# Three output tiles on each normed k-tile, a final norm in token layout, an earlier first weight unit and one table set for log and exp, in a hybrid transformer trunk of depth 2

## The reference, cut to what matters

```python
def rms_norm(x, g):
    x32 = x.astype(F32)
    y = x32 * lax.rsqrt(jnp.mean(x32 * x32, axis=-1, keepdims=True) + NORM_EPS)
    return y.astype(x.dtype) * g

def adaln(cond, w, b):
    m = jax.nn.silu(cond) @ w + b
    return jnp.split(m, 6, axis=-1)

def swiglu(h, w1, w3, w2):
    return (jax.nn.silu(h @ w1) * (h @ w3)) @ w2

# per layer: sh, sc, g of the mixer and of the FFN come from adaln
#   x = x + g1 * (mixer(rms_norm(x, norm1_g) * (1 + sc1) + sh1) @ w_out)
#   x = x + g2 * swiglu(rms_norm(x, norm2_g) * (1 + sc2) + sh2)
# at the end: y = rms_norm(x, final_norm_g), for both token groups
```

## Time and profile before

| what | us |
|---|---|
| median of three runs | 1251.12 (1247.42 to 1253.12) |
| the profiled execution | 1250.76 |
| its span | 1248.9 |
| PE busy with matmuls | 1154.1 |
| POOL, DVE, ACT busy | 541.0, 444.4, 430.8 |

### The profile page before, as it was taken

How to read it: one execution, slowest core, us unless ns; L and a number is a source line. 1 busy time by engine, 2 the same in 40 slices (tenths; PEclk the granted TensorE clock), 3 DMA queues, 4 the chain that set the end, 5 groups by cost and what they waited for, 6 DMA issues and landing times.

```text
span 1248.9 us, 17436 instructions
## 1 busy us (share of the span) xinstructions
PE 1154.1 (92%) x7238; PEld 1047.4 (84%) x7238; DVE 444.4 (36%) x822; ACT 430.8 (34%) x658; POOL 541.0 (43%) x414
## 2 busy tenths in 40 slices
PE   5699998999988999999999989778998999999997
PEld 3399898977767999999999869565597999999996
DVE  4523899215766311111111230428655101111112
ACT  0442422452343423322222242447615333323222
POOL 0344588330015364554455524113043565565662
PEclk9599999989999999999999979889998999999998
DMA  9743323345234666655566642042025444434331
GB/s 311 252 127 104 101 68 102 118 136 189 82 85 138 180 188 185 187 169 170 164 202 184 173 158 68 17 119 68 1 68 135 111 125 135 121 105 117 116 117 51
DMA packets 242940, 163.84 MB, mean 131 GB/s; under 512 B 20214, under 2 KB 241453, under 8 KB 242862
## 3 DMA queue, kind: packets, MB, share of 16 engines
q1 hardware_dynamic: 214880, 135.74, 37.5%
q10 hardware_dynamic: 27982, 26.99, 6.9%
HBM read 159.81 MB, written 2.90 MB: 130 GB/s over the span
## 4 chain that ended last, share of the span: by engine, by line
PE 74%; DVE 12%; ACT 5%; DMA 3%; POOL 3%; issue 2%; ACTq 0%; SPq 0%; DVEq 0%
PE banks L410 19%; PE banks L412 18%; PE banks L411 18%; POOL w_lo L1014 3%; PE banks L484 3%; ACT w_hi L1038 2%; DVE ht L1467 1%; PE banks L450 1%; PE banks L452 1%; PE banks L451 1%; DMA raw<-in_ada_w 1%; DVE h_lo L1458 1%; DVE Qd L1635 1%; DMA raw<-in_w_in_even 1%; DVE Kd L1635 1%
## 5 line engine op out<-in xcount | busy, mean ns | idle before, releaser
L1014 POOL TENSOR_TENSOR w_lo<-raw,w_hi 128x512 fp32r<-128x512 f32 (+2 forms) x410 | 540.8, 1349 | 685.3 <-ACT w_hi L1038 685.3
L410 PE MATMUL banks<-h_hi,w_hi 128*128 128x384 f32 x1152 | 394.6, 343 | 24.4 <-DVE h_lo L1458 16.7
L411 PE MATMUL banks<-h_lo,w_hi 128*128 128x384 f32 x1152 | 388.8, 338 | 0.0
L412 PE MATMUL banks<-h_hi,w_lo 128*128 128x384 f32 x1152 | 388.7, 337 | 0.0
L1038 ACT ACTIVATE w_hi<-raw 128x2048 fp32r<-128x2048 f32 (+4 forms) x115 | 193.4, 1682 | 206.3 <-PE banks L412 157.8
L410 PEld LDWEIGHTS banks<-h_hi,w_hi 128*128 128x128 f32 x1152 | 218.5, 190 | 37.9 <-issue 30.7
L411 PEld LDWEIGHTS banks<-h_lo,w_hi 128*128 128x128 f32 x1152 | 218.7, 190 | 0.7
L412 PEld LDWEIGHTS banks<-h_hi,w_lo 128*128 128x128 f32 x1152 | 218.3, 190 | 0.6
L1510 DVE TENSOR_TENSOR uf<-sa,banks 128x384 f32<-128x384 f32 x44 | 24.4, 554 | 330.2 <-PE banks L412 324.2
L410 PE MATMUL banks<-u_hi,w_hi 128*128 128x384 f32 x352 | 118.8, 338 | 0.9 <-POOL w_lo L1014 0.9
L412 PE MATMUL banks<-u_hi,w_lo 128*128 128x384 f32 x352 | 117.7, 334 | 0.0
(11 more groups left out here) (348 smaller groups left out, 1288.2 us busy)
## 6 DMA issues: line engine op xcount, KB each, us to landing
raw<-in_ffn_w SPq DMA_DIRECT2D x88, 512.0 KB, 5.2
raw<-in_ada_w SPq DMA_DIRECT2D x28, 1024.0 KB, 5.9
raw<-in_ffn_w SPq DMA_DIRECT2D x32, 704.0 KB, 4.6
vada_raw<-in_ada_w ACTq DMA_DIRECT2D x20, 1024.0 KB, 6.7
raw<-in_w_in_even SPq DMA_DIRECT2D x18, 1024.0 KB, 5.2
raw<-in_w_out_even SPq DMA_DIRECT2D x4, 1024.0 KB, 5.7
raw<-in_w_in_odd SPq DMA_DIRECT2D x3, 1024.0 KB, 7.3
raw<-in_w_in_odd SPq DMA_DIRECT2D x8, 256.0 KB, 4.4
```

Source lines behind the costliest of these rows:

```text
L410: pe.matmul(out, s_hi, m_hi, start=first and j == 0, stop=False)
L411: pe.matmul(out, s_hi, m_lo, start=False, stop=False)
L412: mm = pe.matmul(out, s_lo, m_hi, start=False, stop=last and j == len(terms) - 1)
L1014: ins = pool.tensor_tensor(w_lo[s % SPLIT][:, at:to], raw[u % RAW][:, at:to], w_hi[s % SPLIT][:, at:to].bitcast(F32), ALU.subtract)
```

## The change

It has four parts.

1. `first_features` takes three tiles instead of two: in `out0` and `out1` output tiles 0 to 2, in the FFNs gate 0, up 0 and gate 1, in `in1` three `qc` tiles. In `in0` there are still two. The third tile comes from the next unit, `u + 1`. The line that releases unit `u` is unchanged: it names the second tile's completion.
2. The final norm: X's tile m-1 is transposed (`turn_y`, 3 transposes) right after down tile m of layer 1, and DVE multiplies it by the gain row (`take_y`) into `y_tok`, laid over `vada_raw`. `final_norm_g` is broadcast to all partitions by a DMA on ACT's queue. At the end the sum of squares is taken by 6 matmuls with one column each, so the mean stands with tokens on the partitions (128 x 3), and `rstd` scales three rows of 1024: one on ACT, two on DVE, each followed by a DMA.
3. The order at the start: the first `in0` unit ahead of the fourth modulation pair, the second `in0` unit ahead of "norm0"; PE makes modulation "norm0" ahead of the fifth tile of `in0`; DVE and ACT do the lower-bound chain after the norm; ACT splits the second unit after the norm.
4. `norm` loads one table set, `natural_log_exp_and_others`, in place of the dummy log. Over the program ACT has 20 table loads in place of 28.

```diff
-    ada("start")
+    ada("start", range(0, 3))
     add("in0", 1, DT, 256)
+    ada("start", range(3, 4))
+    add("in0", 1, DT, 256, 1)
     ada("norm0")
-    add("in0", 6, DT, 256, 1)
+    add("in0", 5, DT, 256, 2)
...
                 outs = [dense.fill(pe, key)[:, 0:T] for key in keys]
-                unit_ready(u)
                 for k in range(DT):
-                    pe.wait_ge(S["h_ready"], ready + k + 1)
                     for i, out in enumerate(outs):
-                        mm = three(out, [(*weight(u, DT, k, i * P), h_hi[:, k, :], h_lo[:, k, :])], k == 0, k == DT - 1)
+                        if k == 0 and i % 2 == 0:
+                            unit_ready(u + i // 2)
+                        if i == 0:
+                            pe.wait_ge(S["h_ready"], ready + k + 1)
+                        mm = three(out, [(*weight(u + i // 2, DT, k, i % 2 * P), h_hi[:, k, :], h_lo[:, k, :])],
+                                   k == 0, k == DT - 1)
                         if k == DT - 1:
                             mm.then_inc(dense.done, 1)
                 release[u] = (dense.done, dense.at[keys[1]] + 1)
...
+            def turn_y(m):
+
+                dense.was_read(pe, ("down", 1, m))
+                turn(misc, ("y", m), [(c * P, X[:, m, c * P:(c + 1) * P]) for c in range(NCH)])
+
...
-                first_features([("gate", l, 0), ("up", l, 0)], number[(f"up{l}", 0)], ready)
+                first_features([("gate", l, 0), ("up", l, 0), ("gate", l, 1)], number[(f"up{l}", 0)], ready)
                 for f in range(1, FT):
                     u = number[(f"up{l}", f)]
-                    features(("gate", l, f), u, 0)
+                    if f > 1:
+                        features(("gate", l, f), u, 0)
                     features(("up", l, f), u, P)
...
+            turn_y(DT - 1)
+            out = misc.fill(pe, "y_stat")
+            pe.wait_ge(S["sq_ready"], 10)
+            for c in range(NCH):
+                for i in range(2):
+                    mm = pe.matmul(out[:, c:c + 1], sq[:, i, c * P:(c + 1) * P], ones[:, 0:1],
+                                   start=c == 0 and i == 0, stop=i == 1, skip_group_check=True)
...
             def norm(n, base):
-                act.activation(table_col[:, :], eps_col[:, :], ACT.Ln)
+                act.preload_act_table_set("natural_log_exp_and_others")
...
-                if n == 0:
-                    split_to(SPLIT)
...
+            split_to(1)
+            norm(0, 0)
+            split_to(SPLIT)
             act.wait_ge(S["bounds_ready"], 1)
             act.activation(bound_exp[:, 0:2, :], bound_exp[:, 0:2, :], ACT.Exp).then_inc(S["bounds_exp"], 1)
-            split_to(1)
-            norm(0, 0)
...
+            bk = misc.filled(act, "y_stat")
+            step(act.activation(y_rstd, bk[:, 0:NCH], ACT.Ln, bias=eps_col[:, :], scale=1.0 / D))
+            act.activation(y_rstd, y_rstd, ACT.Exp, scale=-0.5).then_inc(S["y_rstd_ready"], 1)
...
+            step(act.activation(y_tok[:, 0, :], y_tok[:, 0, :], ACT.Copy, scale=y_rstd[:, 0:1]))
+            act.dma_start(O[0][0], y_tok[:, 0, :]).then_inc(S["y_sent"], 16)
+            for c in range(1, NCH):
+                act.wait_ge(S["y_ready"], c)
+                act.dma_start(O[1][0][(c - 1) * P:c * P, :], y_tok[:, c, :]).then_inc(S["y_sent"], 16)
```

More of the change, by code:

```diff
@@ L1104, in ffn @@
                     act.activation(u_hi[:, f, :], uf[:, f % 2, :], ACT.Copy).then_inc(S["uhi_ready"], 1)
+                if l == 1:
+                    dense.filled(act, ("up", 1, FT - 1))
+                    with nc.allow_non_contiguous_dma(reason="one row for all partitions"):
+                        act.dma_start(y_g, I["final_norm_g"].partition_broadcast(P)).then_inc(S["g_in"], 16)
                 for m in range(DT):
@@ L1554, in _ @@
                 add_squares(0, m)
+            modulation("start", range(2, 4))
+            biases_to(4)
+            gains(0)
+            norm(0, 0, None)
             b0, b1 = col("hgrn_lower_bounds")[:, 0:8], col("hgrn_lower_bounds")[:, 8:16]
@@ L1564, in _ @@
             step(dve.tensor_scalar(oml[:, :], lb[:, :], -1.0, 1.0, ALU.mult, ALU.add))
-            modulation("start", range(2, 4))
-            biases_to(4)
-            gains(0)
-            norm(0, 0, "norm0")
+            modulation("norm0")
             for d, (f, k) in enumerate(((PF, kf), (SI, kb))):
```

71 lines of the change are left out of this document (39 added, 32 removed).

## The result

The changed kernel takes 1270.8 us (median of four runs, 1268.74 to 1271.12), the kernel before beside it 1252.12 (1247.42 to 1260.44): a ratio of 1.0138, 95% interval 1.0083 to 1.0194. The profiled execution has a span of 1269.2, against 1248.9, so 20.3 us are to be explained between the two traces; the prediction had 13.2. It named the direction and the chief mechanism, and the time lies 2.8 us beyond the upper end of its range.

The account below looks back on a forecast made before the run. TensorE, busy for 92% of the span, was taken as the bound, so only its waits count. Start -1.1, end -3.3, late third units +10.1 and clock +7.5 gave +13.2 on 1250.76: 1264 us, range 1259 to 1267 (0.55).

Parts of the forecast that it names:

- the half clock: Behind five new PE gaps: clock drops, 1.5 us each, +7.5 (bounds 0 and +10); the other answer was no drop.
- the tables of norms 1 and 3: One table load and the dummy log go; DVE and PE wait right behind, so -1.4 us in each norm.
- the late third units: out0, out1, in1 and both FFNs: third unit's split starts 3.65 us later; together +10.1 with starvation and table gains inside.
- the start: First in0 matmul 9.3 us earlier, but later gaps and SP's queue leave net -1.1 at tile 6, between -5 and +1.
- the end: Final norm: tail after the last down matmul shorter by 5.6 us, transposes between down tiles +2.3, net -3.3.
- A: Rival: the stalls come but the clock stays up, 1256.5 us (1255 with the start's gap also harmless); chance 0.17.
- B: Rival: the start keeps its gain, -6 or more at tile 6; with clock up and smaller stalls 1246 us; chance 0.10.
- C: Rival in the FFNs: waiting for gate 0's bank delays gate 2, at most +1 each, 1266 us; chance 0.10 with D.
- D: Rival: every clock drop costs 2.0 us as behind norm 1, the start gains nothing, 1268.5 us; chance 0.10 with C.

Follow-up runs that it names:

- shortened splits: Changed kernel with POOL computing w_lo of the five third units for 512 of 2048 columns only: 1243.94 us, ratio 0.9940 to the kernel before.
- two-tile run: Changed kernel with first_features back at two tiles everywhere; final norm, start and joint table stay: 1246.48 us, ratio 0.9946 to the kernel before.
- pair of runs with POOL shortened: Kernel before without and with the joint table, POOL's w_lo in norms 1 and 3 cut to 512 of 2048 columns: 1251.22 and 1247.03 us.

## Why the prediction was right in direction and 7 us short

The 7.1 us between the predicted 13.2 and the 20.3 of the two traces are: the half clock +2.4, the tables of norms 1 and 3 +2.2, the late third units +1.7, the start +1.3, the rest +0.1, the end -0.6. The steps that failed are the size of the half clock and the table term; the second was wrong in its mechanism too.

- **The late third unit** (predicted +10.1 with the tables inside, +12.9 without): right in the mechanism, 1.7 short; measured +14.6. The span that is left for the preparation was miscounted by one: between matmul 69 and matmul 97 stand 27 matmuls, 4.7 us, not 28. The gaps came at 2.85 to 3.43, also the small one of 0.9 for gate 0's bank. `out0` came at +1.05 for +0.7, `out1` at +3.7 for +3.3, `in1` at +2.2 for +3.0, the FFNs at +3.4 and +4.3 for 3.3 and 2.6. Some of these differences are not the stall: behind norm 3 the half clock lasted for 18 matmuls in place of 9, which is 1.4 of the 1.7 in the second FFN, and behind norm 2 for fewer, 0.7 of `in1`. One sign was wrong: ACT's `w_hi` starts right behind the second tile's end in `out0`, but 2.5 us later in the FFNs, behind the Silu. The shortened splits and the two-tile run both take the loss away whole.
- **The clock behind the gaps** (+7.5, bounds 0 and +10): the right one of the two answers; the term was mis-sized at 1.5 a gap, where 1.4 to 2.8 were measured, 9.9 in all by the landmarks and 9.3 by the windows. I had taken the shorter of the two cases in the trace, arguing that a shorter gap leaves a shorter half clock. It doesn't: 6.0 us at the half clock stand behind 3.43 of idle, 3.0 behind 3.42 in `out1`. The trace of before had a third case, which I left out: behind norm 2 the clock is 0.50 from the first matmul at 729.49 on, for 18 matmuls (it had been there since the small matmuls at 726).

```profile
730.00:731.00 1.00, 1.00 (x5) 1.00 (x4) 0.96 (x4) 0.80 (x2) 0.00 (x0) 0.50 1.08 367
...
735.00:736.00 1.00, 1.00 (x6) 1.00 (x6) 0.96 (x4) 0.36 (x2) 0.00 (x0) 0.79 0.00 0
```

At 0.147 a matmul that is 2.6, and the mean of 2.0, 1.3 and 2.6 is 2.0, which is what the five gaps cost in the mean (9.9 / 5).

- **The tables of norms 1 and 3** (-1.4 each): the step whose mechanism failed. I wrote that DVE and PE wait right behind the exp, which is true, and took DVE's `ht` at its price of before. The row that spoke against it was in the trace of before and not in my sum: `ht` took 1.64 there with POOL's split ending inside it, and the split of this unit runs for 5.0 us from the norm's start, so an `rstd` that comes 1.4 earlier meets it in full. Measured -0.3 each. The pair of runs with POOL shortened shows POOL as the cause of about half of what was missing (0.8 in place of 0.2 comes through), and the modulation pair behind `ht` as the next one.
- **The start** (-1.1, ends -5 and +1): the steps were near. First matmul 43.9 for 45.7, the gap before tile 2 4.46 for 5, tile 6 at 83.6 for 85.4 behind a gap of 3.27. That left a lead of 3.0 at tile 6, not 1.1; that the term is only 1.3 off is partly luck. The sum was wrong since it ended at tile 6: it left out the half clock behind that gap and whether a gap further on would meet one.
- **The end** (-3.3): -3.9, confirmed by its own run. The tail came at -5.8 for -5.6, so the transposes and what goes with them cost 1.9 for 2.3.
- **The rivals.** A, the clock stays: refuted by the windows. B, the start keeps its gain: refuted. C, the wait for gate 0's bank decides gate 2: not as it was put, since that wait was 0.9 and POOL ended the later one of 3.36. But POOL's start followed a split that ACT's own Silu and table load had held for some 2.5 us, so ACT's order had a part in the FFNs; what it costs was not run. D, every drop at 2.0 and nothing from the start, 1268.5, was the closest, and its price of a drop was right in the mean. I gave it and C 0.10 together, and ended the range inside it.
- **The rules of the Trainium skill.** The Trainium skill ("ScalarE: Activation LUTs", "What ACT_TABLE_LOAD costs") has a drain of 1380 ns beside a table load. The trace decides against it as before: in the changed kernel the log starts 1.29 after the load's start, and nothing of 1.38 more appears. The Trainium skill ("TensorE: Matmul & The Clock Gate", "What's actually happening") puts an idle engine at the slower clock. These runs agree for the gaps of 2.85 to 3.43 us ahead of the third units, all of them, and for some of the shorter ones.

## What to carry to other kernels

Sharing an operand among more output tiles keeps the buffers of those tiles longer; before doing it, count the work between the release of the slot and the first use of what must be prepared in it, against the time of the preparation, here 27 matmuls (4.7 us) against 7.7. Look also at what stands ahead of that preparation in its engine's program, here a table load and a Silu. Where a gap of 2 us or more opens on TensorE, reckon with a half clock behind it (1.4 to 2.8 us here), and don't expect an edit that shifts the kernel in time to leave the other gaps at the price they had. When an engine's result comes earlier, look at what its reader will then run beside: here VectorE's `ht` met GpSimd's subtract and took 2.79 in place of 0.75.
